# Mask products behind both logit groups, weight high parts on GpSimd and turned copies on ScalarE in two attentions

## The reference, cut to what matters

```python
# attention A, 16 heads of 64; each position sees its 64 highest-scored keys (2 blocks of 128 queries)
logits = q . k * (A_HEAD_DIM ** -0.5) + bias[head, key - query]
logits = where(valid, logits, NEG);  p = softmax(logits);  out = p @ v;  h = h + out @ w_o
# attention B, 16 heads of 96; a key is seen when its chunk of 64 is not later than the query's
logits = q . k * (QK_DIM ** -0.5)
logits = where(mask, logits, NEG);   p = softmax(logits);  out = p @ v;  h = h + out @ w_o
```

## Time and profile before

| | us |
|---|---|
| median of 3 runs | 1108.05 (1107.82 to 1109.61) |
| the profiled execution | 1110.28 |
| its span, first to last instruction | 1108.2 |
| TensorE busy | 1096.9 (99%) |
| VectorE busy | 760.1 (69%) |
| ScalarE busy | 606.5 (55%) |
| GpSimd busy | 139.4 (13%) |

### The profile page before, as it was taken

One profiled execution on the slowest core, in us unless ns is written; L12 is line 12 of the kernel. 1 busy time (PEld: TensorE's weight loads), 2 busy tenths in 40 slices (PEclk: granted clock), 3 DMA queues, 4 the chain that ended last, 5 costly groups with the idle time before them and its releaser, 6 DMA issues.

```text
span 1108.2 us, 17854 instructions
## 1 busy us (share of the span) xinstructions
PE 1096.9 (99%) x7009; PEld 978.5 (88%) x7009; DVE 760.1 (69%) x1059; ACT 606.5 (55%) x788; POOL 139.4 (13%) x103
## 2 busy tenths in 40 slices
PE   8999999999999999999999999999999999999997
PEld 8868888888998888888889999898899989999996
DVE  5864665656668566656557978576688577988884
ACT  6584544444699654444455546555555357546453
POOL 3633100000273530000030000000000002000003
PEclk9999999999999999999999999999999999999999
DMA  9835565556521356655555654446653566555631
GB/s 298 292 117 106 180 209 193 188 194 225 176 82 45 115 182 196 188 194 188 196 178 164 217 158 130 151 155 213 209 160 127 164 216 228 201 177 192 226 134 39
DMA packets 138929, 194.00 MB, mean 175 GB/s; under 512 B 7163, under 2 KB 113112, under 8 KB 138860
## 3 DMA queue, kind: packets, MB, share of 16 engines
q1 hardware_dynamic: 129004, 184.02, 50.4%
q10 hardware_dynamic: 9248, 8.95, 3.1%
q0 software_dynamic: 608, 0.08, 0.1%
HBM read 191.90 MB, written 6.37 MB: 179 GB/s over the span
## 4 chain that ended last, share of the span: by engine, by line
PE 93%; ACT 4%; DVE 2%; issue 1%; ACTq 0%; DVEq 0%
PE psum L624 22%; PE psum L625 22%; PE psum L626 22%; PE psum L838 11%; PE psum L842 6%; ACT arena L1745 3%; PE psum L712 2%; PE psum L742 1%; PE psum L1388 1%; PE psum L1415 1%; PE psum L1240 1%; PE psum L901 1%; PE psum L902 1%; DVE arena L2698 1%; PE psum L900 1%
## 5 line engine op out<-in xcount | busy, mean ns | idle before, releaser
L2404 DVE TENSOR_TENSOR wlo<-raw,whi 128x2048 fp32r<-128x2048 f32 (+1 forms) x134 | 302.3, 2263 | 136.0 <-ACT whi L1759 134.9
L1759 ACT ACTIVATE whi<-raw 128x2048 fp32r<-128x2048 f32 (+1 forms) x152 | 283.1, 1872 | 174.2 <-PE psum L626 126.0
L624 PE MATMUL psum<-xA,whi 128*128 128x256 f32 x840 | 239.2, 285 | 0.0
L626 PE MATMUL psum<-xA,wlo 128*128 128x256 f32 x840 | 237.6, 283 | 0.0
L625 PE MATMUL psum<-xA,whi 128*128 128x256 f32 x840 | 237.6, 283 | 0.0
L1716 POOL TENSOR_TENSOR wlo<-raw,whi 128x288 fp32r<-128x288 f32 (+3 forms) x43 | 81.8, 1929 | 745.3 <-ACT whi L1759 745.2
L624 PEld LDWEIGHTS psum<-xA,whi 128*128 128x128 f32 x840 | 160.3, 191 | 2.9 <-issue 1.7
L625 PEld LDWEIGHTS psum<-xA,whi 128*128 128x128 f32 x840 | 160.4, 191 | 1.1
L626 PEld LDWEIGHTS psum<-xA,wlo 128*128 128x128 f32 x840 | 160.3, 191 | 0.1
L838 PE MATMUL psum<-xA,whi 128*128 128x512 f32 x512 | 122.5, 391 | 0.0
L624 PE MATMUL psum<-whi,xC 128*128 128x512 f32 (+1 forms) x296 | 114.6, 387 | 0.0
(11 more groups left out here) (308 smaller groups left out, 1697.6 us busy)
## 6 DMA issues: line engine op xcount, KB each, us to landing
raw<-in_w_in SPq DMA_DIRECT2D x42, 1024.0 KB, 5.0
raw<-in_mlp_w_up SPq DMA_DIRECT2D x32, 1024.0 KB, 5.3
raw<-in_mlp_w_down SPq DMA_DIRECT2D x32, 1024.0 KB, 4.8
raw<-in_w_gate SPq DMA_DIRECT2D x11, 1024.0 KB, 5.2
raw<-in_w_up SPq DMA_DIRECT2D x11, 1024.0 KB, 6.5
down_raw<-in_w_down SPq DMA_DIRECT2D x6, 1024.0 KB, 8.1
arena<-in_w_down SPq DMA_DIRECT2D x5, 1024.0 KB, 8.5
raw<-in_b_w_o SPq DMA_DIRECT2D x4, 1024.0 KB, 4.8
```

The lines of the kernel that those rows point to most:

```text
L624: nc.tensor.matmul(out, lh, rh, start=start, stop=False, skip_group_check=skip)
L626: return nc.tensor.matmul(out, ll, rh, start=False, stop=stop, skip_group_check=skip)
L1759: nc.scalar.activation(whi[split_of[c]][:, 0:n], raw_bufs[raw_of[c]][:, 0:n], ACT.Copy).then_inc(hi_sem, 1)
L2404: V.tensor_tensor(wlo[split_of[c]][:, 0:n], raw_bufs[raw_of[c]][:, 0:n], f(whi[split_of[c]][:, 0:n]), ALU.subtract).then_inc(lo_sem["dve"], 1)
```

## The change

Mask products: in A, the logits of both groups and both heads of a pair come first, then one mask product of 384 columns per head; `pick_mask` is laid out in 384 adjacent columns for that. In B, both logit groups of a head come first, then one mask product of 2 x 128 columns. Only a bank's first product has the flag that starts it afresh.

High parts: the five chunks wo1, wo2, bo0, bo1 and bo2 get their high part from GpSimd, in two copies of 1024 columns ahead of the low part there; ScalarE skips them. GpSimd waits for the loaded chunk and for the free buffer itself.

Turned copies: heads 1, 4, 7, 10 and 13 of both attentions are copied by ScalarE. In A the copy of head h-2 stands behind the exponents of head h, in B ahead of them. VectorE skips these copies; in A it waits in their place, at the next head, until the turn has been made, since its next row extreme overwrites that head's exponents.

```diff
+        pool_high = ("wo1", "wo2", "bo0", "bo1", "bo2")
+        act_turns = {"A": (1, 4, 7, 10, 13), "B": (1, 4, 7, 10, 13)}
...
-                                         A["kT"][r0:r0 + 64, 0:w], start=True, stop=False)
-                    for h in pair:
-                        ins = nc.tensor.matmul(psum[:, logit_bank[h % 4], c0:c0 + w], ident_bf[:, :],
-                                               pick_mask[:, blk, 0:w], start=False, stop=True)
-                        if blk == NB - 1:
-                            close_bank(ins, f"A.h{h}.S")
+                                         A["kT"][r0:r0 + 64, 0:w], start=blk == 0, stop=False, skip_group_check=True)
+                for h in pair:
+                    ins = nc.tensor.matmul(psum[:, logit_bank[h % 4], 0:384], ident_bf[:, :], pick_mask[:, :],
+                                           start=False, stop=True, skip_group_check=True)
+                    close_bank(ins, f"A.h{h}.S")
...
-                                     B["kT"][:, h, 0:w], start=True, stop=False, skip_group_check=True)
-                    ins = nc.tensor.matmul(out[:, c0 + w - P:c0 + w], ident_bf[:, :], chunk_mask[:, :],
-                                           start=False, stop=True, skip_group_check=True)
+                                     B["kT"][:, h, 0:w], start=blk == 0, stop=False, skip_group_check=True)
+                ins = nc.tensor.matmul(out[:, 0:512].rearrange("p (a b) -> p a b", b=256)[:, :, 0:128], ident_bf[:, :],
+                                       chunk_mask[:, :].unsqueeze(1).to_broadcast([P, 2, P]), start=False, stop=True,
+                                       skip_group_check=True)
...
-                pool.wait_ge(hi_sem, high[c])
+                if chunks[c]["name"] in pool_high:
+                    pool.wait_ge(raw_sem[raw_of[c]], landed[c])
+                    pool.wait_ge(*chunk_done[prev_split[c]])
+                    for at in range(0, n, 1024):
+                        run(nc.gpsimd.tensor_copy(whi[split_of[c]][:, at:at + 1024], raw_bufs[raw_of[c]][:, at:at + 1024]))
+                else:
+                    pool.wait_ge(hi_sem, high[c])
...
+            def turned(L, h):
+                S = A if L == "A" else B
+                act.wait_ge(*full[f"{L}.h{h}.T"])
+                run(S["PT"][:, h % 2, :], psum[:, bank[f"{L}.h{h}.T"], 0:384], ACT.Copy, read[f"{L}.h{h}.T"])
...
+                    if L == "A" and h - 2 in act_turns["A"]:
+                        turned("A", h - 2)
...
-                if h in (3, 12):
-                    turned_b(h - 2)
+                if h - 2 in act_turns["B"]:
+                    turned("B", h - 2)
...
+                    if L == "A" and h - 1 in act_turns[L]:
+                        dve.wait_ge(*full[f"A.h{h - 1}.T"])
...
-                    if L == "A" or h not in (0, 1, 10):
+                    if h not in act_turns[L] and (L == "A" or h):
                         turned(L, h)
```

More of the change, by code:

```diff
@@ L133, in program @@
         later_mask = sb("later_mask", [P, P], BF16)
-        pick_mask = sb("pick_mask", [P, NB, SEQ], BF16)
+        pick_mask = sb("pick_mask", [P, 384], BF16)
         pick_row = sb("pick_row", [M_HEADS, M_HEADS * P])
@@ L300, in program @@
         last_raw, last_split = {}, {}
-        n_ring, at_split, turn_of = 0, N_SPLIT - 1, None
+        n_ring, n_high, at_split, turn_of = 0, 0, N_SPLIT - 1, None
         for c in range(NC):
@@ L308, in program @@
                 n_ring += 1
-                high[c] = n_ring
+                if chunk["name"] not in pool_high:
+                    n_high += 1
+                    high[c] = n_high
                 name = chunk["name"]
@@ L1807, in split_to @@
                     c = next_split[0]
-                    if not chunks[c]["down"]:
+                    if not chunks[c]["down"] and chunks[c]["name"] not in pool_high:
                         split_static(c)
@@ L1978, in key_mask @@
                 act.wait_ge(*done[f"A.sel{blk}"])
-                run(pick_mask[:, blk, 0:w], A["score"][:, blk, 0:w], ACT.Relu, done[f"A.mask{blk}"], bias=far)
+                run(pick_mask[:, 128 * blk:128 * blk + w], A["score"][:, blk, 0:w], ACT.Relu, done[f"A.mask{blk}"], bias=far)
             def query_half(j):
@@ L2159, in _ @@
                 keys_turned(u)
-            def turned_b(h):
-                act.wait_ge(*full[f"B.h{h}.T"])
-                run(B["PT"][:, h % 2, :], psum[:, bank[f"B.h{h}.T"], 0:384], ACT.Copy, read[f"B.h{h}.T"])
             def between_b(h):
```

## The result

The kernel after takes 1110.86 us (1109.72 to 1112.48, 13 runs); the kernel before, run beside it, takes 1108.18 us (1107.72 to 1109.81, 13 runs). The ratio is 1.0021, with a 95% interval of 1.0013 to 1.0028. The change makes the kernel slower, by 2.3 us by the ratio and 2.7 us between the medians, just over the 2.2 us (0.2%) that the prediction takes as the least that can be told from no change. The profiled execution of the kernel after took 1111.52 us, its span is 1109.4.

What follows compares the result with a forecast made beforehand. The prediction took TensorE, busy 1096.9 of 1108.2 us, to bound the kernel. A +1.6, clock +1.3 and B -1.2 gave +1.7 us, 1109.8 us against the median 1108.05; range 1107.7 to 1111.7 us.

Steps and rivals of the forecast that it cites:

- The hold-up: In A, ScalarE's late copy of head 1 keeps bank 7 full; TensorE starts the logits of heads 6 and 7 3.5 us late.
- What comes back in A: After the stall, mask gains and 1.37 us of vanished waits leave A 1.6 us slower, bounds 1.0 to 3.0.
- The clock: Behind the stall in A, TensorE's granted clock falls and costs 1.3 us, bounds 0 and 1.7.
- Masks in A: Mask products in A gain 0.10 us a pair, 0.8 us over eight pairs, bounds 0 to 0.21 a pair.
- Masks in B: Mask products in B gain 0.11 us a head, of which nine heads' worth, 1.0 us, remains.
- B as a whole: Attention B is 1.2 us faster, bounds 0.5 and 1.8: 1.0 from masks, about 0.2 from ScalarE's splits and VectorE's copies.
- GpSimd's copies: High parts on GpSimd take at most about 4.6 us a chunk, the dear end taken, and cost nothing either way.
- (1): The stall in A comes but the clock stays up: +0.4 us, 1108.5 us; chance 0.22.
- (2): ScalarE's remaining A copies also come late, up to 1 us each; two make +1.9, 1111.7 us; chance 0.16.
- (3): No stall in A because bank 7 is somehow free: 1104.8 us; chance 0.06.

Runs made afterwards that it cites:

- e1: The kernel before with only head 1's turned copy in A moved to ScalarE, behind the exponents of head 3: 1114.19 us, ratio 1.0050 to before.
- e2: The kernel after with head 1's copy in A back on VectorE: 1107.82 us, ratio 0.9997 to before.
- e8: The kernel after with head 1's copy in A issued earlier on ScalarE, ahead of scaling pair 2's queries: 1107.28 us, ratio 0.9991 to before.
- e4: The kernel after with fifteen products of no use on TensorE while it waits at bank 7: 1107.80 us, ratio 0.9998 to before.
- e9: The kernel after with only heads 7, 10 and 13 of A copied by ScalarE, heads 1 and 4 by VectorE: 1105.07 us, ratio 0.9969 to before.
- e7: The kernel after with the five high parts back on ScalarE: 1113.10 us, ratio 1.0039 to before.
- e5: The kernel before with the new order of logits and mask products alone: 1107.96 us, ratio 0.9999 to before.
- e11: The kernel after with masks as before and no copy of A by ScalarE: 1107.04 us, ratio 0.9986 to before.
- e3: The kernel after with all five turned copies of A back on VectorE: 1107.04 us, ratio 0.9983 to before.

## Why the prediction was right, and which terms were off

The forecast of 1109.8 us, slower by one hold-up in A, came out as 1110.86 us, just above the forecast's own bounds (1109.0 to 1110.8) and inside the stated range. It put more chance on "within 0.2%" than on "slower"; the result lies just past that line. By its own steps:

- **The hold-up.** Right. From the first logits of A, the text has bank 7's transposes at 70.03 - 57.30 = 12.73 us; they came at 69.42 - 56.76 = 12.66. e1 and e2 show it is that one copy; e8 shows it is its place in ScalarE's order.
- **What comes back in A.** Nearly right. With the clock kept up (e4) A is 1.29 us slower, where the text has 1.6. From the logits behind the stall to the second output product e4 takes 97.36 - 69.95 = 27.4 us against 27.8. Two errors cancel in part here, which is luck: the masks gave more than priced (0.31 us a pair, below), and some 0.7 of the 1.37 us of waits stayed.
- **The clock.** Right in kind, and the term of the sum that was most mis-sized: 1.3 us (bounds 0 and 1.7) against 2.5 between e4 and the kernel after. The price was read from the one gap of the earlier trace rows, of 1.83 us, and a gap of twice that length was said to do the same. It did more: 0.50 from the end of the stall to about 75 us. In e1, behind the same 3.68 us, it lasted to 80 and cost about 6 us, so the length of the gap doesn't set the length of the half clock by itself. Nor does it decide whether the clock falls: that gap near the start has a price in six of the fourteen profiled executions only, and it was luck that the one read was of these. In e9 TensorE is idle there just as long and goes on at full clock (timeline, then stretches; beside the earlier trace rows):

```profile
9.26 0.69 PE L985 MATMUL psum<-whi,xA 128*128 128x200 f32 x4 [1.86 <-ACT whi L1755]
```

```profile
9.26:15.86 6.60, 6.27 (x49) 5.68 (x50) 5.86 (x7) 5.82 (x12) 1.93 (x4) 1.00 0.79 237
```

What decides is left open by these runs. The half clock followed in all three traces with an idle stall of 3.68 us (after, e1, e7). The Trainium skill, in TensorE: Matmul & The Clock Gate, Part 1, has activity release the throttle; e4 agrees, since activity without use kept the clock at 1.00.

- **Masks in A.** Mis-sized: in the undisturbed pair 82.72 to 83.91 is 1.19 us for logits and masks, against 1.50 in the earlier trace rows: a gain of 0.31 us a pair where the text has 0.10, with 0.21 as the upper bound. It took the fixed price of a change between 64-row and full products from the masks' slots alone. The logits fell as well, from 0.42 + 0.64 = 1.06 to 0.86 us, which points to a price on both sides of a change; no run separates it from other causes. TensorEngine Tiling (Array Packing) in the Trainium skill, under Key Properties, says that a change of the tiling mode drains the array. That agrees in kind; the 0.31 us is from here. (The text's "four logits" are two products, since the view lists an fp32 product twice.) Yet the sum came to 0.14 us alone (e5) and 0.75 with the helpers relieved (e11 to e3), not to 8 x 0.31 = 2.5: TensorE's own slots were not what ended last, the waits for its helpers were.
- **Masks in B.** Right in size: before, head and first output slot take 359.88 - 358.83 = 1.05 us (from the earlier trace rows to the row at 359.88 above), now 362.20 - 361.27 = 0.93, so 0.12 against 0.11. The head alone takes 0.77 us, where the text has 0.71. More than half of the gain, 0.07, lies in the output's first slot, and where the text keeps nine heads of it, 0.08 us shows alone (e5) and 0.56 with the helpers relieved.
- **B as a whole.** 1.2 forecast, 1.11 measured, right in sum and wrong in its parts, which is luck. The text gives 1.0 to the masks and 0.2 to the helpers. The runs give 0.08 to the masks alone, 0.22 to GpSimd alone, 0.54 to GpSimd and copies together, and a loss of 0.96 to masks and copies without GpSimd. The parts are worth something only together, and a sum of terms can't show that.
- **GpSimd's copies.** The dear end of 4.6 us a chunk was wrong: 2.14 us, near ScalarE's 1.91. The Trainium skill's page GPSIMD Engine Reference, section 4.1, calls one-input work there roughly line rate, and was nearer. The dear end made no difference to the sum, since by the text's count the low part was early enough either way. What the text missed is that taking the splits away from ScalarE is worth 1.3 us in A and 2.1 in B once ScalarE has the copies (e7).
- **The rivals.** (1), full clock: fell to the 0.50 above, and e4 shows what it would have been, 1107.8. (2), later copies late too: not in the kernel after, but in e2 and e8 as 1.23 us at head 4, over the "up to 1 us" that the text gives. (3), no hold-up, 1104.8: e8, with all ten copies and without it, took 1107.3, since head 4's copy comes late in it. With that copy gone too (e9) A and B are 2.6 us shorter than before, near the 3.3 that this rival adds up.

## What to carry to other kernels

Before work moves to a less busy engine, read where the moved instruction stands in that engine's order, and which buffer it empties: here half a microsecond behind two heads' exponents held up the busiest engine for 3.7 us. Price a long wait of TensorE twice, once for the wait and once for the work at half clock behind it, the second as a range, and read it from more than one execution. Where the wait can't be taken away, products without use in it can pay. A gain in TensorE's slots counts only while no helper is late, so relieve the helpers first and measure the parts together as well as alone.

## What the runs showed of the hardware

- The same idle time of 3.68 us was followed by half clock for some 5.5 us in one execution (after) and 12 in another (e1). Shorter idle times went both ways: 1.23 us (e2) was followed by a mean of 0.61 over 4 us, 1.38 us (e7) by 1.00; near the start 1.83 us by 0.74 (before) and 1.86 us by 1.00 (e9). Waits of up to 0.6 us (e5, e9) cost no clock.
- GpSimd rounds 128 x 2048 fp32 numbers to the high part in 2.14 us (two operations of 1024 columns), under half of the 4.51 us that the subtraction with two inputs takes for as many.
- Grouping the 64-row logits of a pair ahead of its full products, with two mask products in place of four, saves 0.31 us a pair, 0.20 of it in the logits.
